# A two-block decoder kernel with gathered experts: embedding work one unit earlier, gate halves in expert slots, keys of the sliding attention in other banks

## The reference

```python
x = x + peer_ffn(x, ...)           # layers peer0, peer1
x = ple_add(x, p[i], ...)          # layers ple0, ple1
k, v = shared_kv(x, ...)           # after ple0: "kv"
x = x + swa_sink_attention(x, ..., k, v)   # layer swa, between ple0 and peer1
return rmsnorm(x, final_norm)

def peer_ffn(x, ...):   # 16 experts per row and head, 8 heads, rows of tables u and v
    a = einsum('nd,nhkd->nhk', h, u[idx]);  w = gate * gelu(a)
    return einsum('nhk,nhkd->nd', w, v[idx])

def ple_add(x, p_i, norm_g, proj, gate_w):
    gate = sigmoid(rmsnorm(x, norm_g) @ gate_w)
    return x + (p_i @ proj) * gate
```

## Time and profile before

| | |
|---|---|
| median of 3 executions | 2757.41 us (2756.09 to 2761.15) |
| the profiled execution | 2753.48 us, its span 2751.7 us |
| PE busy / DVE / ACT / POOL | 90% / 69% / 43% / 31% of the span |
| layer peer0, first gather issued to last landed | about 1273 to 1923 us |
| ple0 and swa, up to peer1's first gather | about 1925 to 2057 us |
| layer peer1, gathers | about 2057 to 2717 us |
| ple1 and the end | about 2718 to 2752 us |

### The profile page before, as it was taken

The page is one execution under the profiler, slowest core; times in us unless marked ns, Lnnn a source line. Parts: engine busy times, 40 slices in busy tenths (PEclk is TensorE's granted clock), DMA queues, the critical chain, the costliest instruction groups (busy, mean ns, idle before and its releaser), DMA issues.

```text
span 2751.7 us, 32201 instructions
## 1 busy us (share of the span) xinstructions
PE 2464.5 (90%) x10416; PEld 1675.6 (61%) x10416; DVE 1902.5 (69%) x3840; ACT 1178.2 (43%) x2586; POOL 857.9 (31%) x700
## 2 busy tenths in 40 slices
PE   8999999999899999998899777779888898787788
PEld 7888788888778878986444333334764444233234
DVE  7885588888668875655667767666567676766664
ACT  4446744544574456563333322333453333333334
POOL 0005400000230026664333333443433333333443
PEclk9999999999999999999999999889999999988999
DMA  6554355555425544448999999999549999999995
GB/s 212 188 177 138 128 194 186 180 191 184 148 90 189 190 153 138 154 153 353 419 416 418 417 418 409 418 413 395 178 153 419 419 419 418 413 419 415 413 415 239
DMA packets 141953, 783.39 MB, mean 285 GB/s; under 512 B 15873, under 2 KB 16385, under 8 KB 76289
## 3 DMA queue, kind: packets, MB, share of 16 engines
q0 software_dynamic: 73728, 536.90, 47.2%
q1 hardware_dynamic: 65360, 237.44, 25.7%
q10 hardware_dynamic: 2736, 7.46, 0.9%
HBM read 780.69 MB, written 1.05 MB: 284 GB/s over the span
## 4 chain that ended last, share of the span: by engine, by line
PE 47%; DMA 24%; DVE 9%; ACT 7%; issue 7%; POOL 6%; POOLq 0%; ACTq 0%; SPq 0%; DVEq 0%
DMA arena<-experts,arena 24%; PE ps L703 11%; PE ps L681 6%; PE ps L682 6%; PE ps L683 6%; PE ps L704 5%; PE ps L1283 5%; PE ps L1286 5%; POOL ring_lo L387 4%; DVE arena L2687 2%; POOL arena L2804 2%; ACT row L1887 2%; ACT arena L1880 1%; ACT L1878 1%; DVE ring_lo L387 1%
## 5 line engine op out<-in xcount | busy, mean ns | idle before, releaser
L2687 DVE SCALAR_TENSOR_TENSOR arena<-arena,ps 128x1024 f32<-128x1024 f32 x512 | 617.5, 1220 | 385.1 <-DMA arena<-experts,arena 383.6
L1283 PE MATMUL ps<-arena,row 128*128 128x512 f32 x1024 | 570.1, 640 | 207.5 <-ACT row L1887 207.5
L2804 POOL DMA_INDIRECT arena<-experts,arena x512 | 483.4, 944 | 772.2 <-PE ps L1286 512.5
L1286 PE MATMUL ps<-arena,row 128*128 128x512 f32 x1024 | 553.9, 623 | 0.0
L381 ACT ACTIVATE ring_hi<-ring 128x1024 fp32r<-128x1024 f32 x416 | 437.7, 1058 | 177.7 <-PE ps L683 140.3
L703 PE MATMUL ps<-hT,ring_hi 128*128 128x512 f32 x1408 | 503.4, 400 | 3.4 <-DVE hT L2208 3.2
L1283 PEld LDWEIGHTS ps<-arena,row 128*128 128x128 f32 x1024 | 197.5, 201 | 487.3 <-ACT row L1887 279.3
L387 POOL TENSOR_TENSOR ring_lo<-ring,ring_hi 128x1024 fp32r<-128x1024 f32 x143 | 346.3, 2432 | 282.3 <-ACT ring_hi L381 261.6
L704 PE MATMUL ps<-hT,ring_lo 128*128 128x256 f32 x1408 | 395.8, 281 | 0.0
L1286 PEld LDWEIGHTS ps<-arena,row 128*128 128x128 f32 x1024 | 206.7, 202 | 269.0 <-issue 269.0
L387 DVE TENSOR_TENSOR ring_lo<-ring,ring_hi 128x1024 fp32r<-128x1024 f32 x273 | 331.9, 1239 | 20.5 <-ACT ring_hi L381 19.9
(11 more groups left out here) (341 smaller groups left out, 3553.8 us busy)
## 6 DMA issues: line engine op xcount, KB each, us to landing
ring<-stream SPq DMA_DIRECT2D x424, 512.0 KB, 3.4
arena<-experts,arena POOLq DMA_INDIRECT x512, 13.2
row<-rows_in ACTq DMA_DIRECT2D x11, 512.0 KB, 4.9
arena<-stream SPq DMA_DIRECT2D x8, 512.0 KB, 5.0
queries_in_ring_hi<-stream SPq DMA_DIRECT2D x8, 512.0 KB, 6.2
queries_in_w<-stream SPq DMA_DIRECT2D x4, 512.0 KB, 7.5
queries_in_h_lo<-stream SPq DMA_DIRECT2D x4, 512.0 KB, 5.4
x<-x_in SPq DMA_DIRECT2D x1, 1024.0 KB, 4.8
```

Of the source, the lines that this page charges most:

```text
L1283: lower = pe.matmul(ps[:, 2 * tb, :], diag, v[:, 0:HALF], start=first, stop=end)
L1286: pe.matmul(ps[:, 2 * tb + 1, :], diag, v[:, HALF:D], start=first, stop=end)\
L2687: last = dve.scalar_tensor_tensor(u, u, 1.0, h, ALU.mult, ALU.mult, accum_out=R["a"][:, n % 2, k:k + 1])
L2804: pool.indirect_dma_start(R["held"][:, g % HELD, :], None, experts, bass.IndirectOffsetOnAxis(ap=idx[:, n % 2, k:k + 1], axis=0))\
```

## The change

1. **HELD_AT.** The eleven expert slots start at element 8088 of the arena; before, they followed the regions ahead of them and started at 8084.
2. **One unit earlier.** Projection and transposes of row block 0 go from unit 14 to 13, DVE's and ACT's parts of it too; the gate products with gate 0 to 3 go from unit 15 to units 14 (two) and 15 (two). POOL makes the low parts of gate 2 and 3 between gathers of unit 15, no longer after the last.
3. **LAST_GATES.** High and low part of gate 4 to 7 are kept in the expert slots of picks 245 to 248, so that they don't wait for `ring_hi` and `ring_lo` slots; the ring slots after them are free earlier. SP loads gate 4 to 7 when pick 253 has landed. ACT makes the high part of gate 4 first of all in `ple(l)`, POOL no longer waits for x there, and PE multiplies row block 0 with gate 4 ahead of row block 1 with gate 0 to 3.
4. **swa.** Keys and values go to banks 2 and 3. The mean is made after the key input's parts; DVE empties the banks between the fourth and fifth query input part; PE waits for that only before row block 1 of the first query block. ACT makes the squares before the high parts of `swa_q`, and POOL the power before its low parts.
5. **The end.** DVE updates x fully before it scales; four pieces, four stores of 128 x 512.

```diff
+HELD_AT = 8088
-EARLY_GATE = {(PH + 7, 1): 0, (PH + 7, 2): 1, (PH + 7, 4): 2, (PH + 7, 5): 3}
+LAST_GATES = {AT[f"ple{l}_gate"] + 4 + i: PICKS * (l + 1) - HELD + i for l in range(2) for i in range(4)}
+EARLY_GATE = {(PH + 6, 2): 0, (PH + 6, 3): 1, (PH + 7, 0): 2, (PH + 7, 1): 3}
...
+        def part(b):
+            if b in LAST_GATES:
+                hi_lo = rounded("gate_parts", HELD_AT + LAST_GATES[b] % HELD * EXPERT, 2, BLK)[0]
+                return hi_lo[:, 0], hi_lo[:, 1]
+            return ring_hi[:, b % SLOTS, :], ring_lo[:, b % SLOTS, :]
...
+            elif b in LAST_GATES:
+                act.wait_ge(of("expert_free"), LAST_GATES[b] + 1)
+            elif b - SLOTS in LAST_GATES:
+                act.wait_ge(used, b - 2 * SLOTS + 1)
...
-                    sp.wait_ge(of("expert_free"), HELD_BACK[b])
+                    pick_of = HELD_BACK[b]
+                    sp.wait_ge(expert_landed[pick_of % HELD], 16 * (pick_of // HELD + 1))
...
-            for b in range(TB):
-                sp.wait_ge(of("result"), 1 + 2 * b)
-                sp.dma_start(out[b * P:(b + 1) * P, :], arena[:, b * D:(b + 1) * D]).then_inc(out_done, 16)
+            for n, (b, c) in enumerate((b, slice(h * HALF, (h + 1) * HALF)) for b in range(TB) for h in range(2)):
+                sp.wait_ge(of("result"), n + 1)
+                sp.dma_start(out[b * P:(b + 1) * P, c], xn[:, b, c]).then_inc(out_done, 16)
...
-                        last = products(ps[:, tb, 0:256], h_tiles(k, tb),
+                        last = products(ps[:, 2 + tb, 0:256], h_tiles(k, tb),
...
-                if (n, group) == (PH + 6, 0):
+                if (n, group) == (PH + 5, 0):
...
+                wait_split(pe, first + TAIL)
+                for half in range(2):
+                    gate_product(l, TAIL, 0, half)
...
-                    for k in range(TAIL, KD):
+                    for k in range(TAIL + (b == 0), KD):
...
+                    if name == "swa" and k == 3:
+                        make_hi(act, AT["swa_q"] + 1)
+                if name == "kv":
+                    squares_of_block(BEFORE[name], 1, ss_ready)
+                    make_hi(act, AT["swa_q"])
...
-                if (n, group) in ((PH + 7, 0), (PH + 7, 1)):
+                if (n, group) in ((PH + 6, 0), (PH + 6, 1)):
                     make_hi(act, AT[f"ple{l}_gate"] + 2 + group)
...
+                make_hi(act, AT[f"ple{l}_gate"] + TAIL)
...
-                    dve.wait_ge(rs_ready, mean(0, EPS))
-                    scaled(n, 0)
+                    first_stat = mean(0, EPS)
                     update(2)
...
+                    scaled(n, 0, slice(0, HALF))
+                    second_stat = mean(1, EPS)
+                    scaled(n, 0, slice(HALF, D))
...
-                    if n == PH + 7:
+                    if n == PH + 6:
                         ple_low_parts(0, of("ple_hT0_a"), KD * l, of("ple_hT0_d"))
...
-                for k in range(2, TAIL):
-                    make_lo(pool, AT[f"ple{l}_gate"] + k)
+                        if n == PH + 7 and group in (0, 1):
+                            make_lo(pool, AT[f"ple{l}_gate"] + 2 + group)
...
-                wait_x(pool, BEFORE[name], 2)
+                if not name.startswith("ple"):
+                    wait_x(pool, BEFORE[name], 2)
```

More of the change, by code:

```diff
@@ L711, in ring_parts, with split_row_blocks @@
             def ring_parts(b, c):
-                return ring_hi[:, b % SLOTS, c], ring_lo[:, b % SLOTS, c]
+                hi, lo = part(b)
+                return hi[:, c], lo[:, c]
             def by_rows(dst, tile, b, half, start, stop):
                 return products(dst, tile, ring_parts(b, slice(half * 512, half * 512 + 512)), start, stop)
-            def split_row_blocks(first, n, banks=0, tiles=h_tiles, entering=None):
+            def split_row_blocks(first, n, banks=0, tiles=h_tiles, entering=None, second=None):
                 for k in range(n):
@@ L723, in split_row_blocks @@
                     for b in range(TB):
+                        if k == 0 and b == 1 and second is not None:
+                            second()
                         for half in range(2):
@@ L1948, in ple @@
                 layer = LAYERS.index(f"ple{l}")
-                for b in range(TAIL, KD):
+                squares_of_block(layer - 1, 1, ss_ready)
+                for b in range(TAIL + 1, KD):
                     make_hi(act, AT[f"ple{l}_gate"] + b)
-                    if b == TAIL:
-                        squares_of_block(layer - 1, 1, ss_ready)
                 x_stat = made[0]
@@ L2209, in norm_in @@
                                              ALU.mult, ALU.subtract).then_inc(hT_d, 1)
+                    if name == "swa" and k == 3:
+                        kept_kv(means_of_kv)
                 if name.startswith("ffn"):
@@ L2213, in norm_in, with kept_kv @@
                     make_lo(dve, AT[name] + 3)
+            def kept_kv(stat):
+                R = attention_regions(1)
+                dve.wait_ge(rs_ready, stat)
+                dve.wait_ge(used, AT["swa_kv"] + 2)
+                own_wait("swa")
+                for tb in range(TB):
+                    last = dve.scalar_tensor_tensor(R["kv"][:, tb, :], ps[:, 2 + tb, 0:256], rs[:, tb:tb + 1], R["kv_b"],
+                                                    ALU.mult, ALU.add)
+                last.then_inc(of("swa_kv"), 1)
             def kept_row(name, bank_at):
@@ L2460, in swa @@
                 norm_in("kv")
-                norm_in("swa")
-                dve.wait_ge(rs_ready, means_of_x())
-                dve.wait_ge(used, AT["swa_kv"] + 2)
-                own_wait("swa")
-                for tb in range(TB):
-                    last = dve.scalar_tensor_tensor(R["kv"][:, tb, :], ps[:, tb, 0:256], rs[:, tb:tb + 1], R["kv_b"],
-                                                    ALU.mult, ALU.add)
-                last.then_inc(of("swa_kv"), 1)
+                norm_in("swa", means_of_x())
                 dve.wait_ge(of("swa_kv"), 1)
@@ L2864, in _ @@
                 first, done, end = AT[FIRST_PART[name]], SLOTS + 2 if name.startswith("ple") else 1, POOL_BLOCKS[name][0]
-                ahead = min(end, done + (1 if name.startswith(("ple", "ffn")) else 3))
+                ahead = min(end, done + (1 if name.startswith(("ple", "ffn")) or name == "kv" else 3))
                 lows(first + done, first + ahead)
```

51 lines of the change are left out of this document (28 added, 23 removed).

## The result

Four executions of the changed kernel took 2740.07 to 2742.43 us, median **2741.33 us**, against 2757.07 for four of the kernel before: ratio 0.9939, 95% interval 0.9927 to 0.9950, or 16.8 us less (13.8 to 20.1); the medians are 15.7 apart. Forecast were 10.7 us less, 2746.5; the forecast's own range was 2742 to 2751, and rival D widened it down to 2739.5. So the sign held, the wider range held and the narrower one was missed by 0.7 us; 5 to 6 us are missing from the sum.

The account below looks back on a forecast made before the run. Gathers (DMA) were taken to bound the expert layers, so savings lie in PE's waits outside them: 2.0 + 3.3 - 1.0 + 5.4 + 1.0 = 10.7 us off 2757.4, rounded 2746.5 us. Own range 2742 to 2751, with rivals 2739.5 to 2753.

Parts of the forecast that it names:

- rival D: Expert gathers: slots aligned to 32 bytes make them 0.4% faster, 5.1 us more saved, 2741.6 us; chance 0.10.
- The moved slots (part 1) I cost at nothing: Expert layers' gathers: moving the slots by four elements was given no saving and no cost.
- 0.8 us in each layer: End of each expert layer: moving projection and gate products earlier removes PE's 0.8 us lateness at the last values.
- -1.0 us: Last gathers of both layers: the earlier loads of gate 4 to 7 delay them by 0.5 us a layer.
- (A): Last gathers: the gate loads delay them by 4 us a layer instead of 0.5, 2753.7 us; chance 0.10.
- Gate 4 to 7: ple0 and ple1: row block 0 of the gate ready sooner, saving 2.0 us (backlog's 0.8 included) and 3.3 us.
- swa, "5.4 us": swa before the query products: PE's pause goes, 4.0 us, and the low clock behind it, 1.4 us.
- (C): swa: PE waits for POOL's low part at every query block, losing some 4 us again, 2750.7 us; chance 0.13.
- The end, "1.0 us": End of the kernel: update ahead of scaling saves 0.8 us, half-size last store 0.2 us.
- (B): Units 13 to 15: the gather queue runs dry, 9 us lost a layer, 2764.7 us; chance 0.04.
- (E): Gate products: a high part still waits and PE's stalls only change their name, 2757 us; chance 0.03.

Follow-up runs that it names:

- e1: The kernel before with only the expert slots moved, to element 8088 instead of 8084: 2753.94 us against 2758.09, ratio 0.9988.
- e2: The kernel before with only the expert slots moved, to element 8092, still 16 bytes off a step of 32: 2754.01 us, ratio 0.9988.
- e9: The kernel before with only the expert slots moved, to element 8100: 2753.47 us, ratio 0.9984.
- e10: The kernel before with the expert layers' regions moved up by 32 bytes, slots with them to 8092: 2754.30 us, ratio 0.9985.
- e8: The kernel before with only projection, transposes and gate products one unit earlier and low parts of gate 2 and 3 between gathers: 2758.68 us, ratio 1.0002.
- e11: e7 with the last four picks of a layer each a group of its own: 2740.17 us against 2757.09 for the kernel before, ratio 0.9933.
- e7: The changed kernel with gate 4 to 7 loaded when pick 254 has landed, one gather later: 2739.63 us, ratio 0.9939 to the kernel before.
- e6: The changed kernel with gate 4 to 7 loaded as before, when PE has freed pick 252: 2740.71 us, ratio 0.9938 to the kernel before.
- e3: The kernel before with only the swa changes (banks 2 and 3, means and squares moved, DVE's emptying between query parts): 2751.58 us, ratio 0.9976.
- e4: The kernel before with only the changes at the end (x updated before scaling, four pieces, four stores): 2759.28 us, ratio 1.0002.
- e5: The changed kernel run once more, unaltered: 2740.37 us against 2757.87 for the kernel before, ratio 0.9941.

## Why the prediction was right, and where not

**Right in sign, and low by about 5.5 us, most of it one term set at nothing.** The measured 2741.33 us lies under the forecast's own range (2742 to 2751), and within the wider one only because that took in rival D, whose mechanism the runs refute. So that the range held is in part luck.

- *"The moved slots (part 1) I cost at nothing":* this step failed. Moving the slots alone saves 3.3 to 4.4 us in four kernels (e1, e2, e9, e10), in the profiles 2.0 in peer0 and some 1 in peer1. Rival D, at 0.10, had this term, and its time of 2741.6 is the measured one within 0.3. That is luck: its 5.1 us are too much for the slots, the rest came from other terms, and its mechanism is wrong: 8092, as far off a step of 32 bytes as 8084, is fast.
  The page cited there (the Trainium skill, "DMA: Bandwidth & Descriptors", How a descriptor splits into AXI transactions) also has the first transaction start at the boundary of 256 bytes below the descriptor's start, which the prediction left out of its 256 and 257 beats. In this kernel the arena begins at byte 97760 of a partition, so 8084 lies 48 bytes past such a boundary, 8088 64, 8092 80, 8100 112. An estimate by the whole of that page's rule is 258, 258, 259 and 260 beats a row, so never fewer. The page tells of bytes that are read, and the slots are written, so it may not bear on them; the measurement has the slow place first, and it decides.
- *"0.8 us in each layer" for the backlog:* this step failed too. The products moved forward change nothing (e8: last values 3.05 after the dots, 3.04 before). In e11 the late start went with the pair of picks: two picks are four halves of 0.86 us, started together behind the second pick's landing, and with pick 254 PE has six halves, 5.2 us, ahead of the last values.
- *"-1.0 us" for the loads:* the mechanism was right and the size near (0.65 and 0.61 of delay for my 0.5), and even the sign of (A) showed up, a gap over 3 us. But it costs almost nothing, because it lies behind that same backlog of PE (e7). The two steps failed in opposite directions and met. The Trainium skill's rule that a DMA engine goes round its queues by whole packets (same page, Queues, rings and completion order) would, as an estimate, have put the delay at about 2 us more for both layers than I took; the delay seen was 0.3 us more for both.
- *Gate 4 to 7:* right in size. From the undelayed landing, ple0 saves 19.45 - 17.70 = 1.75 us where my terms gave 2.0 - 0.5, ple1 20.69 - 17.65 = 3.0 where they gave 3.3 - 0.5. In sum 4.8 for 4.3. Part 2 alone gives nothing (e8) and the earlier load 0.4 in ple0 (e6), so the rest comes from part 3 or from the two together; no run has part 3 alone, and its pieces (parts in slots, order on PE, POOL's wait) weren't tried apart. POOL was not in the way before: its low parts of gate 2 and 3 had ended at 1910.97 (22.30 us ahead of 1933.27), 14 us ahead of the last diagonal.
- *swa, "5.4 us":* the mechanism was right, the size some 0.7 low. The pause of 3.89 is gone and the clock is at 1.00 where it was 0.94; e3 saves 6.6 (4.1 to 9.1) by the runs. By the pair of profiles, 109.6 us from sigmoid to peer1's first gather in the changed kernel against 114.8 before is 5.1; but that execution was the shortest of eight without part 4, whose mean is 115.8, against 109.5 for the six with it. From the last key product to the first query product it was 4.17 us and is 0.12, and the query products take 2.0 less in the mean (e3), where the prediction took 1.4: 6.1 together. (C) fell: POOL kept ahead.
- *The end, "1.0 us":* 0.90 from the last gate piece on (0.96 in e4). Of it 0.16 went back between the first sigmoid and the last (5.60 for 5.44).
- (B) did not happen: DMA share 1.01 in the stretch 1800 to 1900. (E) neither: PE has no idle time within the gate products.

Sum by what was measured: 3 to 4.4 (slots) + 4.8 (ple0, ple1) + 6.1 to 6.6 (swa) + 0.75 (end) = 14.7 to 16.6 us, against 16.8 (13.8 to 20.1) and 16.3 (12.7 to 20.1) by the runs. So of the 5 to 6 us missing, the slots are 3 to 4.4, swa 0.7 to 1.2, ple0 and ple1 0.5.

## What to carry to other kernels

In a stretch that the DMA bounds, the address at which a gather lands is a parameter worth trying by itself: three other offsets are one line each. Before a backlog is put down to the work that was added, count what the engine gets in one piece at the end (here a pair of picks); and a delay ahead of an engine with a queue is paid only as far as it is longer than the queue. A cost of nothing given to an edit that only moves an address needs a row as much as any other term. What a low clock costs behind a pause differs from execution to execution (1.5 to 2.9 us here), so it wants more than one profile. And a rival that hits the time isn't thereby right: its own mechanism has to be tried, as e2 did with D's.

## What the runs showed of the hardware

- Gathers of 128 rows of 8192 bytes took 0.3% longer (659.1 against 657.1 us for the 256 of peer0) with slots at element 8084 or 9108 than at 8088, 8092 or 8100. The two slow places are 4096 bytes apart, which suits an effect that repeats with the address, with a period of 4096 bytes or a part of it; 8100 is 64 bytes past 8084 and fast, so not 64 or a part of it. Two slow places don't prove a period. Which it is, and why, stays open.
- Four ring loads of 0.5 MB, issued when pick 253 had landed, delayed pick 255 by 0.61 to 0.66 us, not by their own 5.0 us; issued one gather later, by nothing.
- A pause of TensorE of 2.2 us was followed by a lowered granted clock (0.62 to 0.81 in the 3 us stretches of e8) in two of five executions (e8, e6) and by 1.00 in three (the changed kernel, e5, e7), at the same place of nearly the same program.
- A pause of 3.9 us ahead of the query products was followed by a lowered clock in all eight executions that had it: 0.88 to 0.94 over those products (1.00 in the six without the pause), and 1.5 to 2.9 us.
